# Output projection of a decoder block: seven products with sums replaced by eight plain ones, and two expert homes loaded earlier

## The chip, the cores and the metric

One core of one Trainium2 chip runs the whole program. The metric is the device time of one execution in microseconds, the median of the runs. All arithmetic is float32.

## What is computed

One decoder block on 256 tokens of width 1024, with a sparse attention (NSA) and a retention as token mixers and a mixture of 32 experts behind them. What matters here is the joint between the two halves:

```python
x = x + W_o( sigmoid(gA) * (yA @ W_upA) + sigmoid(gB) * (yB @ W_upB) )
x = x + HierMoE(RMSNorm(x))   # coarse top-1 group of 4, then top-2 of its 8 experts
```

Each of the 32 experts has gate and up weights of 1024x256 each (2 MB together) and down weights of 256x1024 (1 MB). All 32 are streamed from memory once per execution, 96 MB in all, whichever tokens chose them.

## The kernel before

**Order of the work.** The kernel is written by hand, one instruction stream for each engine, with semaphores between them. Each result of TensorE (PE) is a *job* in one of 8 PSUM banks; the list END_JOBS (L104) gives the bank of each job of the last part before the experts. A job is full when PE is done with it, and emptied when another engine has read it. The order of the calls in each engine's stream is the order in which it works; an engine that waits holds all that stands behind it.

**Token tiles and quarters.** The 256 tokens are two tiles of 128 (t = 0, 1), the 1024 columns two halves of 512 (n = 0, 1). A `product` (L693) is a sum over k-slices of 128: four matmuls of 128x128 by 128x512.

**Projections by seven products.** The gate and up projections (groups vr, gr, ga, gb, un, ur) and the output projection (out) each compute a 2x2 block product with seven products in place of eight (Winograd's form of Strassen's scheme). For it DVE makes four sums of weight quarters (T1 to T4) and four sums of quarters of the left operand, and further sums put the products together. In the group out the jobs are outX (first and second product), outZ (fifth), outW (sixth and seventh), outQ (fourth) and out3 with out4 (third product, in two pieces of 256 columns). ACT keeps the first product (`keep_first("out")`, L1396), POOL adds it to three quarters of x (L637 to L640), and DVE adds the others (L1940 to L1970). Token tile 1 comes ahead in the groups ur and out.

**Around it.** DVE's `merge(t, n)` (L1888) adds the two gated mixers in gate_a; PE transposes the result in four jobs mT00 to mT11 (`merged_transposes`, L1009), ACT copies them to mergedT (L1374), which lies in the region called keys. When a piece of x has its output sum, ACT sums its squares (L1400), POOL weights it for the experts (L628), PE transposes it in the jobs x2T00 to x2T12 (`stream_transposes`, L1051), and ACT copies them to h2T (L1410). PE's `route(t)` multiplies h2T with the router weights; DVE's `router(t)` (L1997) turns the logits into the tokens' choices by a chain of small operations; `places(t)` (PE L1065, DVE L1984) numbers the tokens of each expert. Then PE's `gather` (L1115) picks the tokens of the first four experts with a selection matrix, first from tile 0, then, after places(1) and counts, from tile 1.

**The experts.** Batches of four experts: gate and up products GU0 to GU3 (jobs GU0.c and on), tanh, products, down products O0.c and O1.c, and a combination into four PSUM banks which were seeded with x (`seed`, ACT L1422). Expert e's gate-up weights lie in home e mod 6, its down weights in home e mod 8 (L383 to L388). The homes are regions that the first half of the kernel uses for other things: ring slots, xs, x, keys, windows, qkT and others.

**The loads.** All large loads are issued from the queue of SyncE (SP), in one order, each behind a wait for its home (L465 to L529). `first_gu(e)` and `first_dw(e)` load expert e's weights into an empty home; `reload_gu(e)` waits until GU of expert e - 6 is full, `reload_dw(b)` until O0.c and O1.c of batch b - 2 are. The weights of the output projection lie in two blocks, out0 in ring slot 2 and out1 in the region vr_and_gr.

Of the kernel before, what the change touches and what calls it, by code (L numbers as in the profile page):

```python
# [12 lines left out]
P = 128  # L13
# [33 lines left out]
def shape_tables():  # L47

    def onehot(dist):
# [54 lines left out]
END_JOBS = [("urX", 3), ("urV", 4), ("urZ", 5), ("urW", 7), ("mT10", 2), ("mT11", 1), ("outX", 6), ("mT01", 0), ("mT00", 2),  # L104
            ("outZ", 5), ("outW", 7), ("outQ", 4), ("x2T10", 2), ("out3", 3), ("x2T00", 0), ("out4", 1), ("x2T01", 2),
            ("route0", 0), ("x2T11", 3), ("x2T12", 1), ("route1", 3), ("pos0", 2), ("pos1", 3), ("counts", 0)]
# [11 lines left out]


NTH = dict(vr=1, gr=2, ga=3, gb=4, un=5, ur=6, out=7)  # L120
# [28 lines left out]
def build(nc, a, out):  # L149
    with ExitStack() as ctx:  # L150
# [109 lines left out]
        mergedT = r_kpad[:, :].rearrange("p (k t) -> p k t", k=KT)  # L260
        ya_sums = q_and_ya[:, 0:1024].rearrange("p (s k n) -> p s k n", s=4, k=2)
        yr_sums = [attention[:, i * 512:(i + 1) * 512].rearrange("p (k n) -> p k n", k=4) for i in range(4)]
        second_aside = xs[:, :, :].rearrange("p t (k n) -> p (t k) n", k=2)

        m0 = nsa[:, 0:4096]
        selG = m0[:, 0:256].rearrange("p (t e s) -> p t e s", t=TT, e=BE)
        selW = m0[:, 256:512].rearrange("p (t e s) -> p t e s", t=TT, e=BE)
        selWT = m0[:, 512:768]
        hg = m0[:, 768:1792].rearrange("p (k s) -> p k s", k=KT)
        gu_sb = m0[:, 1792:2816].rearrange("p (b n) -> p b n", b=2)  # L270
# [3 lines left out]
        h2T = nsa[:, 2048:4096].rearrange("p (k t) -> p k t", k=KT)  # L274
# [7 lines left out]
        out_sums = [gate_a[:, t, n * 512:n * 512 + 512].rearrange("p (k n) -> p k n", k=4) for t, n in ((1, 0), (0, 1), (0, 0), (1, 1))]  # L282
# [39 lines left out]
        s_S, s_aS, s_rS, s_oS = sem("h_sums"), sem("attention_sums"), sem("retention_sums"), sem("merged_sums")  # L322
        s_x_P1, s_ga, s_gb = sem("first_product_added"), sem("attention_gate_tanh"), sem("retention_gate_tanh")
# [20 lines left out]
        def quarters(group):  # L344

            if group in ("ur", "out"):
                w = [slot(f"{dict(ur='upr', out='out')[group]}{i}").rearrange("p (k n) -> p k n", k=4) for i in range(2)]
# [7 lines left out]
        def left(v, one=0):  # L355

            n = v.shape[1] // 2
            a, b = (slice(t * P, (t + 1) * P) for t in (one, 1 - one))
            return v[:, 0:n, a], v[:, n:2 * n, a], v[:, 0:n, b], v[:, n:2 * n, b]
# [4 lines left out]
        def results(group):  # L364
# [4 lines left out]
            one = 1 if group == "ur" else 0  # L369
            return v[:, one, 0:512], v[:, one, 512:D], v[:, 1 - one, 0:512], v[:, 1 - one, 512:D]  # L370

        def piece_ready(piece):

            return dict(out0=(s_P7_read, NTH["out"]), out1=is_emptied("outW"), out2=is_emptied("outX"), out3=is_emptied("out3"),
                        out4=is_emptied("out4"))[piece]
# [51 lines left out]
        def _(sp):  # L427
# [42 lines left out]
            first_dw(2)  # L470
            sp.wait_ge(s_y, TT)
# [13 lines left out]
            first_dw(6)  # L485
            sp.wait_ge(s_P7, NTH["ur"])
# [74 lines left out]
        def _(pool):  # L561
# [93 lines left out]
        def _(pe):  # L655
# [327 lines left out]
            r11, r12, r21, r22 = left(yrT, 1)  # L983
# [28 lines left out]
            merged_transposes(1, 0, 1)  # L1012
# [4 lines left out]
            merged_transposes(1, 1, 2)  # L1017
            m11, m12, m21, m22 = left(mergedT, 1)
            b11, b12, b21, b22 = quarters("out")
            oX = begin("outX")  # L1020
            have("mT10")
            for b in ("out0", "out1"):
                pe.wait_ge(*loaded(b))
            product(oX[:, :], m11, b11, True, False).then_inc(s_P1, 1)
# [3 lines left out]
            merged_transposes(0, 1, 3)  # L1028
            have("mT11")
            pe.wait_ge(s_P1_kept, NTH["out"])  # L1030
            product(oX[:, :], m12, b21, False, False, range(2))
            merged_transposes(0, 0, 4)
            done("outX", product(oX[:, :], m12, b21, False, True, range(2, 4)))
            oZ = begin("outZ")
            pe.wait_ge(s_T1, NTH["out"])
            pe.wait_ge(s_oS, 1)
            done("outZ", product(oZ[:, :], out_sums[0], b12))
            oW = begin("outW")
            pe.wait_ge(s_oS, 2)
            pe.wait_ge(s_T2, NTH["out"])  # L1040
            product(oW[:, :], out_sums[1], second_aside, True, False).then_inc(s_P6, 1)
            oQ = begin("outQ")
            have("mT01")
            pe.wait_ge(s_T4, NTH["out"])
            done("outQ", product(oQ[:, :], m22, b21))
            pe.wait_ge(s_oS, 3)
            pe.wait_ge(s_T3, NTH["out"])
            pe.wait_ge(s_P6_read, NTH["out"])
            done("outW", product(oW[:, :], out_sums[2], b11, False, True))
# [28 lines left out]
            stream_transposes("x2T10")  # L1078
            o3, o4 = begin("out3"), begin("out4")
            pe.wait_ge(s_oS, 4)  # L1080
            done("out3", product(o3[:, 0:256], out_sums[3], b22[:, :, 0:256]))
            stream_transposes("x2T00")
            product(o4[:, 0:256], out_sums[3], b22[:, :, 256:512], True, False, range(2))
            stream_transposes("x2T01")
            done("out4", product(o4[:, 0:256], out_sums[3], b22[:, :, 256:512], False, True, range(2, 4)))
# [4 lines left out]
            stream_transposes("x2T12")  # L1090
# [150 lines left out]
        def _(act):  # L1241
# [52 lines left out]
            def keep_first(group):  # L1294

                act.wait_ge(s_P1, NTH[group])
                dst, scale = (x_squared, 0.5) if group == "out" else (results(group)[2], 1.0)
                nc.scalar.activation(dst, ps(f"{group}X")[:, :], ACT.Copy, scale=scale).then_inc(s_P1_kept, 1)
# [914 lines left out]
```

## Time and profile before

| | |
|---|---|
| median of 3 runs | 505.08 us (503.76 to 505.58) |
| the profiled execution | 502.69 us |
| its span in the profile | 500.7 us |
| PE busy | 469.1 us, 94% |
| DVE busy | 225.7 us, 45% |
| ACT busy, POOL busy | 89.9 us, 40.7 us |
| moved by DMA | 151.33 MB, mean 302 GB/s |
| mean granted clock of PE | 0.957 |

Each engine's busy time is the sum of its instructions; the span runs from the first instruction to the last. A busy PE need not be at full rate: the granted clock is 1.00 at 2.4 GHz and 0.50 at 1.2 GHz, and a float32 matmul shows as two instructions, so that a product of four k-slices is 8 in the views. Releasers of waits are inferred.

### The profile page before, as it was taken

Reading aid. Unit: us, or ns where it says so; the run is one execution under the profiler, and the core shown is the slowest. Engines: PE = TensorE matmul, PEld = TensorE weight load, DVE = VectorE, ACT = ScalarE, POOL = GpSimd, SP = SyncE. Lnnn points to the kernel's source line nnn. Section 1 sums busy time; section 2 is a strip of 40 time slices with the busy share of each in tenths; the row PEclk is TensorE's granted clock in tenths of the full one; section 3 lists DMA queues with packets and bytes.
Section 4 is the critical chain, followed back from the end, with each engine's and each line's share of the span. In section 5 each row is a group of like instructions: output and inputs, shape, how many; then the busy total and the mean of one; then the engine's idle time right before and its main releaser. Section 6 shows DMA issues by size and latency. Waiting matters only on the chain.

```text
span 500.7 us, 6261 instructions
## 1 busy us (share of the span) xinstructions
PE 469.1 (94%) x2434; PEld 259.2 (52%) x2434; DVE 225.7 (45%) x511; ACT 89.9 (18%) x244; POOL 40.7 (8%) x62
## 2 busy tenths in 40 slices
PE   5999999999999999999989889999999998979873
PEld 2499745564555545544435846464563636437320
DVE  1563019928766578779684651222231311111203
ACT  1000006214341110100101712021111211011012
POOL 0700050500000001000132300000000000000001
PEclk9999999999999999999989888999999996987987
DMA  8998679326025019489783989999999999999972
GB/s 262 418 377 206 207 283 375 130 61 277 0 84 254 0 63 418 191 346 418 276 344 111 395 327 429 400 428 428 407 432 414 426 427 408 431 408 432 417 292 88
DMA packets 20860, 151.33 MB, mean 302 GB/s; under 512 B 2947, under 2 KB 3396, under 8 KB 14172
## 3 DMA queue, kind: packets, MB, share of 16 engines
q1 hardware_dynamic: 19296, 147.88, 72.9%
q0 software_dynamic: 1296, 2.92, 2.9%
q8 instruction: 22, 0.36, 0.3%
q10 hardware_dynamic: 236, 0.08, 0.1%
q14 instruction: 10, 0.08, 0.0%
HBM read 148.25 MB, written 2.62 MB: 301 GB/s over the span
## 4 chain that ended last, share of the span: by engine, by line
PE 73%; DMA 17%; DVE 5%; SPq 2%; issue 2%; ACT 0%; POOLq 0%; POOL 0%; DVEq 0%; ACTq 0%
PE bank L672 33%; PE bank L697 29%; DMA ring<-in_moe_gate_up 10%; DMA attention_small<-in_moe_down 6%; PE bank L1127 4%; PE bank L1100 4%; PE bank L703 2%; SPq L453 1%; DMA ring<-in_dense 1%; SPq L457 1%; DVE ring L1616 0%; DVE nsa L1528 0%; DVE nsa L1890 0%; DVE nsa L1886 0%; DVE nsa L2068 0%
## 5 line engine op out<-in xcount | busy, mean ns | idle before, releaser
L2068 DVE COPY nsa<-bank 128x512 f32<-128x512 f32 x32 | 22.1, 691 | 97.3 <-PE bank L672 71.7
L697 PE MATMUL bank<-ring,x 128*128 128x512 f32 x128 | 57.3, 594 | 0.0
L672 PE MATMUL bank<-ring,nsa 128*32 128x512 f32 x336 | 43.1, 638 | 5.6 <-DMA ring<-in_moe_gate_up 5.6
L672 PEld LDWEIGHTS bank<-cst,nsa 128*128 128x128 f32 x256 | 34.4, 213 | 24.5 <-issue 16.6
L1462 ACT ACTIVATE nsa<-bank 128x512 f32<-128x512 f32 (+1 forms) x40 | 22.2, 554 | 127.3 <-PE bank L672 104.7
L697 PE MATMUL bank<-ring,hT_and_y 128*128 128x512 f32 x96 | 43.4, 597 | 0.0
L672 PE MATMUL bank<-cst,nsa 128*128 128x32 f32 x256 | 37.2, 298 | 1.2 <-DVE nsa L2068 1.2
L697 PEld LDWEIGHTS bank<-ring,x 128*128 128x128 f32 x128 | 23.8, 190 | 27.6 <-issue 27.5
L1127 PE MATMUL bank<-nsa,Tb 128*128 128x128 f32 x256 | 36.1, 308 | 1.0 <-DVE nsa L1994 1.0
L1127 PEld LDWEIGHTS bank<-nsa,Tb 128*128 128x128 f32 x256 | 35.4, 225 | 1.2 <-issue 1.2
L2078 DVE SCALAR_TENSOR_TENSOR cst<-cst,bank 128x64 f32<-128x64 f32 x32 | 7.1, 221 | 58.0 <-ACT cst L1470 58.0
L1100 PE MATMUL bank<-nsa 128*128 128x512 f32 x64 | 29.9, 607 | 0.8 <-ACT nsa L1462 0.8
L672 PE MATMUL bank<-hT_and_y,ring 128*128 128x256 f32 x128 | 28.2, 380 | 0.2 <-issue 0.2
L697 PEld LDWEIGHTS bank<-ring,hT_and_y 128*128 128x128 f32 x96 | 17.6, 190 | 20.1 <-issue 20.1
L672 PEld LDWEIGHTS bank<-hT_and_y,ring 128*128 128x128 f32 x128 | 24.1, 190 | 4.0 <-DVE hT_and_y L1547 0.8
L672 PEld LDWEIGHTS bank<-ring,nsa 128*32 128x32 f32 x336 | 9.5, 111 | 26.4 <-issue 20.1
L1699 DVE CUSTOM_DVE_ANT_0 nsa<-bank,Tb 128x128 f32<-128x128 f32 (+1 forms) x32 | 9.6, 354 | 28.9 <-DMA Tb<-bias_rows 26.9
L672 PE MATMUL bank<-ring,hT_and_y 128*128 128x128 f32 (+2 forms) x96 | 22.0, 388 | 0.0
L672 PE MATMUL bank<-ring,Tb 128*128 128x512 f32 x32 | 16.9, 688 | 5.3 <-DMA ring<-in_dense 5.3
L1100 PEld LDWEIGHTS bank<-nsa 128*128 128x128 f32 x64 | 11.3, 189 | 20.0 <-issue 19.5
L1274 ACT ACTIVATE nsa<-nsa,mneg 128x128 f32<-128x128 f32 (+1 forms) x32 | 14.1, 443 | 26.1 <-DVE mneg L1528 26.1
L651 POOL TENSOR_TENSOR st<-st 128x1 f32<-128x1 f32 x2 | 1.6, 778 | 208.8 <-DVE st L2134 208.8
(274 smaller groups left out, 690.8 us busy)
## 6 DMA issues: line engine op xcount, KB each, us to landing
ring<-in_moe_gate_up SPq DMA_DIRECT2D x21, 2048.0 KB, 19.6
ring<-in_dense SPq DMA_DIRECT2D x17, 2048.0 KB, 12.1
hT_and_y<-in_moe_gate_up SPq DMA_DIRECT2D x6, 2048.0 KB, 17.6
vr_and_gr<-in_moe_gate_up SPq DMA_DIRECT2D x5, 2048.0 KB, 22.7
windows<-in_moe_down SPq DMA_DIRECT2D x8, 512.0 KB, 17.9
nsa<-in_moe_down SPq DMA_DIRECT2D x8, 512.0 KB, 19.4
queries_and_attention<-in_moe_down SPq DMA_DIRECT2D x8, 512.0 KB, 24.3
attention_small<-in_moe_down SPq DMA_DIRECT2D x8, 512.0 KB, 19.4
```

The lines of the kernel that those rows point to most:

```text
L453: sp.dma_start(GU[i].rearrange("p k w f -> p (k w f)"), expert(gate_up_v, j, e)).then_inc(s_gu[i], 16)
L457: sp.dma_start(DW[i][:, h, :, :].rearrange("p k n -> p (k n)"), expert(down_v[:, h, :, :], j, e)).then_inc(s_dw[i][h], 16)
L672: return nc.tensor.matmul(o, l, r, start=s, stop=e)
L697: ins = nc.tensor.matmul(o, l[:, k, :], r[:, k, :], start=first and k == 0, stop=last and k == n - 1, skip_group_check=True)
L703: ins = nc.tensor.transpose(o[:, i * P:(i + 1) * P], s, ident)
L1100: return nc.tensor.matmul(bank[4 + q][:, 0:w], l, r, start=s, stop=e, skip_group_check=True)
L1127: ins = nc.tensor.matmul(o[:, k * P:(k + 1) * P], xe[:, t, (4 * h + k) * P:(4 * h + k + 1) * P], selG[:, t, :, :].rearrange("p e s -> p (e ...
L1274: ins = nc.scalar.activation(p, p, ACT.Exp, bias=mneg[:, t, h, b:b + 1], accum_out=sums[:, t, h, b:b + 1])
L1462: nc.scalar.activation(dst, bank[k][:, src], ACT.Copy).then_inc(emptied[k], 1)
L1699: ins = V.tensor_tensor_reduce(dst, o[:, b * S:b * S + w], Tt[:, h, S - w:S], 1.0, -3e38, ALU.add, ALU.max, mx[:, t, h, b:b + 1])
L2068: V.tensor_copy(dst, bank[k][:, src]).then_inc(emptied[k], 1)
L2078: V.scalar_tensor_tensor(h, t, 1.0, bank[k][:, 0:2 * C], ALU.add, ALU.mult).then_inc(s_hch, 1)
```

## The change

The output projection is computed piece by piece: for each of the pieces out0 (tile 0, columns 0 to 511), out1 (tile 0, the rest), out2 (tile 1, columns 0 to 511), out3 and out4 (tile 1, 256 columns each) the product over all eight k-slices, in two halves of four (`output`). The weight sums, the left sums, the kept first product and POOL's additions are gone, and so is the aside copy of a weight sum in xs. Tile 0 is now ahead in ur and out. mergedT lies in gate_b, each quarter where the gate quarter was, so the keys region is free after the retention and xs after the un group: the down weights of expert 3 (home keys) are loaded behind job Y11, and those of expert 4 (home xs) behind the first merge. The blocks out0 and out1 now hold column halves in place of row halves. The working area of the experts in nsa is laid out in another order.

Cut to its core:

```diff
@@ SP's queue @@
             first_dw(2)
+            sp.wait_ge(*is_full("Y11"))
+            first_dw(3)
             sp.wait_ge(s_y, TT)
...
             first_dw(6)
+            sp.wait_ge(s_mrg, 1)
+            first_dw(4)
             sp.wait_ge(s_P7, NTH["ur"])
...
             first_dw(1)
-            sp.wait_ge(s_P6, NTH["out"])
-            sp.wait_ge(s_T4, NTH["out"])
-            first_dw(4)
-            sp.wait_ge(*is_full("outW"))
+            sp.wait_ge(*is_full("out2"))
             first_gu(4)
-            sp.wait_ge(*is_full("outQ"))
-            sp.wait_ge(s_oS, 4)
-            first_dw(3)
             sp.wait_ge(*is_full("out4"))
             first_gu(5)
@@ POOL @@
-            pool.wait_ge(s_P1_kept, NTH["out"])
-            for t, c0 in ((0, 0), (0, 512), (1, 512)):
-                pool.wait_ge(s_x[t], 32)
-                xx = x[:, t, c0:c0 + 512]
-                pool.tensor_tensor(xx, xx, x_squared, ALU.add).then_inc(s_x_P1, 1)
             pool.wait_ge(s_nffn, 16)
+            weighted("out0")
+            weighted("out1")
+            router_rstd(0)
             weighted("out2")
-            weighted("out0")
-            router_rstd(0)
-            weighted("out1")
             weighted("out3")
@@ PE @@
-            merged_transposes(1, 1, 2)
-            product(oX[:, :], m11, b11, True, False).then_inc(s_P1, 1)
...
+            merged_transposes(0, 1, 2)
+            def output(o, t, kh, c0, c1):
+                w = cols(f"out{c0 // 512}", 512)[:, 4 * kh:4 * kh + 4, c0 % 512:c0 % 512 + c1 - c0]
+                return product(o[:, 0:c1 - c0], mergedT[t][kh], w, kh == 0, kh == 1)
+            o0 = begin("out0")
+            have("mT00")
+            pe.wait_ge(*loaded("out0"))
+            output(o0, 0, 0, 0, 512)
             pe.wait_ge(s_T4, NTH["ur"])
             pe.wait_ge(s_P7_read, NTH["ur"])
             done("urW", product(uW[:, :], r22, u21, False, True))
...
+            merged_transposes(1, 1, 3)
             have("mT01")
+            done("out0", output(o0, 0, 1, 0, 512))
+            o1 = begin("out1")
+            pe.wait_ge(*loaded("out1"))
+            output(o1, 0, 0, 512, D)
+            merged_transposes(1, 0, 4)
...
+            stream_transposes("x2T00")
+            done("out1", output(o1, 0, 1, 512, D))
+            o2 = begin("out2")
+            have("mT10")
+            output(o2, 1, 0, 0, 512)
             stream_transposes("x2T01")
+            have("mT11")
+            done("out2", output(o2, 1, 1, 0, 512))
             pe.wait_ge(s_wr, 1)
             have("x2T00", "x2T01")
             route(0, range(KT))
+            o3 = begin("out3")
+            output(o3, 1, 0, 512, 768)
+            stream_transposes("x2T10")
+            done("out3", output(o3, 1, 1, 512, 768))
+            o4 = begin("out4")
+            output(o4, 1, 0, 768, D)
+            places(0)
             stream_transposes("x2T11")
+            done("out4", output(o4, 1, 1, 768, D))
             have("x2T10")
             route(1, range(4))
             have("x2T11")
             route(1, range(4, 6))
+            stream_transposes("x2T12")
             have("x2T12")
             route(1, range(6, KT))
-            places(0)
@@ ACT @@
+            act.wait_ge(s_gb, 4)
             keep_first("ur")
+            merged_out(0, 0)
+            merged_out(0, 1)
+            merged_out(1, 1)
             merged_out(1, 0)
-            keep_first("out")
...
+            squares(0, "out0")
+            turned("x2T00")
+            squares(1, "out1")
+            turned("x2T01")
+            squares(2, "out2")
             turned("x2T10")
+            normed(0)
+            seed(1)
             squares(3, "out3")
             turned("x2T11")
+            exps_router(0)
             squares(4, "out4")
             turned("x2T12")
             seed(0)
+            normed(1)
             exps_router(1)
             seed(2)
             seed(3)
@@ DVE @@
-            first_sum_of_out()
-            second_sum_of_out()
             last_product("ur")
...
-            left_sums(mergedT, out_sums, s_oS, 1)
-            third_sum_of_out()
-            third_left_sum(mergedT, out_sums, s_oS, 1)
-            fourth_sum_of_out()
...
+            residual("out0")
+            residual("out1")
+            variance(0)
+            residual("out2")
             dve.wait_ge(s_ms, 2)
+            router(0)
+            residual("out3")
+            places(0)
+            residual("out4")
             partial_variance()
-            router(0)
             variance(1)
-            places(0)
             router(1)
             places(1)
```

## Rows read from the trace of the kernel before

**Rows 1.** The page's slices of 12.5 us: busy share of the DMA engines, and what they moved.

```profile
DMA  8998679326025019489783989999999999999972
GB/s 262 418 377 206 207 283 375 130 61 277 0 84 254 0 63 418 191 346 418 276 344 111 395 327 429 400 428 428 407 432 414 426 427 408 431 408 432 417 292 88
```

**Rows 2.** Stretches: us, busy time by engine, then clock, DMA share and GB/s.

```profile
287.30:289.40 2.10, 1.78 (x16) 1.69 (x16) 0.58 (x3) 1.00 (x2) 0.00 (x0) 0.99 0.17 35
294.40:483.00 188.60, 177.56 (x1260) 95.88 (x1264) 40.89 (x124) 28.12 (x70) 0.00 (x0) 0.92 1.01 419
483.00:500.60 17.60, 8.47 (x40) 2.14 (x32) 4.34 (x8) 4.07 (x10) 1.56 (x2) 0.79 0.26 100
```

**Rows 3.** SP's queue in order of time: start, us, issue.

```profile
243.96 0.33 SPq L453 DMA_DIRECT2D ring<-in_moe_gate_up  x1
...
288.33 0.80 SPq L457 DMA_DIRECT2D x<-in_moe_down  x2
...
292.73 0.33 SPq L453 DMA_DIRECT2D hT_and_y<-in_moe_gate_up  x1
...
312.24 0.33 SPq L457 DMA_DIRECT2D windows<-in_moe_down  x1
```

**Rows 4.** The chain that ended last, in order of time: start, us, what.

```profile
210.19 29.20 PE bank L697 x68
...
273.14 0.44 PE bank L703 x4
273.58 1.73 PE bank L697 x8
...
277.93 1.96 PE bank L672 x16
```

**Rows 5.** PE in order of time: start, us, group, and the pause ahead of it.

```profile
243.76 0.60 PE L703 MATMUL bank<-cst,nsa 128*128 128x128 f32 x4
...
255.34 0.66 PE L703 MATMUL bank<-cst,nsa 128*128 128x128 f32 x4 [1.95 <-DVE nsa L1890]
...
280.69 1.95 PE L672 MATMUL bank<-wr,nsa 128*128 128x36 f32 x16 [0.35 <-ACT nsa L1250]
...
284.08 3.58 PE L1127 MATMUL bank<-nsa,Tb 128*128 128x128 f32 x16 [0.70 <-DVE nsa L1994]
287.49 0.31 PE L672 MATMUL bank<-member,cst 128*128 128x32 f32 x2
...
288.79 2.02 PE L1127 MATMUL bank<-nsa,Tb 128*128 128x128 f32 x16 [0.32 <-DVE nsa L1994]
290.74 1.92 PE L672 MATMUL bank<-hT_and_y,nsa 128*32 128x512 f32 x16
```

**Rows 6.** Stretches around the half clock; third value from the end is the granted clock.

```profile
241.50:244.30 2.80, 2.80 (x11) 1.44 (x10) 0.40 (x2) 0.00 (x0) 0.00 (x0) 1.00 0.02 7
...
256.60:260.00 3.40, 3.40 (x5) 1.35 (x4) 3.21 (x3) 0.03 (x1) 0.00 (x0) 0.50 0.94 383
...
283.90:287.30 3.40, 3.22 (x15) 3.25 (x16) 2.70 (x16) 2.62 (x8) 0.00 (x0) 0.50 0.96 402
287.30:290.70 3.40, 3.08 (x27) 2.92 (x26) 0.58 (x3) 1.60 (x3) 0.00 (x0) 0.99 0.42 136
...
297.50:304.40 6.90, 6.90 (x36) 2.44 (x28) 1.43 (x5) 0.22 (x1) 0.00 (x0) 0.51 0.99 423
```

**Rows 7.** DVE in order of time: start, us, instruction.

```profile
240.87 0.69 DVE L1890 TENSOR_TENSOR nsa<-nsa 128x512 f32<-128x512 f32 x1
...
253.65 1.63 DVE L1890 TENSOR_TENSOR nsa<-nsa 128x512 f32<-128x512 f32 x1
...
275.35 0.42 DVE L1938 SCALAR_TENSOR_TENSOR x<-bank,x 128x256 f32<-128x256 f32 x1 [0.88 <-PE bank L697]
...
283.93 0.22 DVE L2003 SCALAR_TENSOR_TENSOR rt<-bank,st,rbias 128x4 f32<-128x4 f32 x1
...
286.51 0.25 DVE L2018 SCALAR_TENSOR_TENSOR member<-cst,rt 128x32 f32<-128x32 f32 x1
```

More of the change, by code:

```diff
@@ L102 @@
 BANK0 = 5
-END_JOBS = [("urX", 3), ("urV", 4), ("urZ", 5), ("urW", 7), ("mT10", 2), ("mT11", 1), ("outX", 6), ("mT01", 0), ("mT00", 2),
-            ("outZ", 5), ("outW", 7), ("outQ", 4), ("x2T10", 2), ("out3", 3), ("x2T00", 0), ("out4", 1), ("x2T01", 2),
-            ("route0", 0), ("x2T11", 3), ("x2T12", 1), ("route1", 3), ("pos0", 2), ("pos1", 3), ("counts", 0)]
+END_JOBS = [("urX", 3), ("urV", 4), ("urZ", 5), ("urW", 7), ("mT00", 2), ("mT01", 1), ("out0", 6), ("mT11", 0), ("out1", 5),
+            ("mT10", 2), ("x2T00", 1), ("out2", 4), ("x2T01", 3), ("route0", 0), ("out3", 1), ("x2T10", 2), ("out4", 3),
+            ("pos0", 1), ("x2T11", 0), ("route1", 0), ("x2T12", 2), ("pos1", 3), ("counts", 0)]
 PIECES = dict(out0=(0, 0, 512), out1=(0, 512, 1024), out2=(1, 0, 512), out3=(1, 512, 768), out4=(1, 768, 1024))
 TURNED = dict(x2T00=("out0", 0, 4), x2T01=("out1", 4, 8), x2T10=("out2", 0, 4), x2T11=("out3", 4, 6), x2T12=("out4", 6, 8))
-NTH = dict(vr=1, gr=2, ga=3, gb=4, un=5, ur=6, out=7)
+NTH = dict(vr=1, gr=2, ga=3, gb=4, un=5, ur=6)
 BATCH_C = ["GU0.c", "GU1.c", "T0.c", "GU2.c", "T1.c", "GU3.c", "T2.c", "T3.c", "WT.c"]
@@ L344, in quarters @@
         def quarters(group):
[L346 to L347 removed]
+            if group == "ur":
+                w = [slot(f"upr{i}").rearrange("p (k n) -> p k n", k=4) for i in range(2)]
                 return w[0][:, :, 0:512], w[0][:, :, 512:1024], w[1][:, :, 0:512], w[1][:, :, 512:1024]
@@ L353, in quarters, with left @@
             return w[0][:, 0:4, :], w[1][:, 0:4, :], w[0][:, 4:8, :], w[1][:, 4:8, :]
-        def left(v, one=0):
+        def left(v):
             n = v.shape[1] // 2
-            a, b = (slice(t * P, (t + 1) * P) for t in (one, 1 - one))
-            return v[:, 0:n, a], v[:, n:2 * n, a], v[:, 0:n, b], v[:, n:2 * n, b]
+            return [v[:, k * n:(k + 1) * n, t * P:(t + 1) * P] for t in range(TT) for k in range(2)]
         def weights_of(group):
@@ L368, in results @@
                 v = r_qkT[:, :].rearrange("p (t d) -> p t d", t=TT)
-            one = 1 if group == "ur" else 0
-            return v[:, one, 0:512], v[:, one, 512:D], v[:, 1 - one, 0:512], v[:, 1 - one, 512:D]
+            return v[:, 0, 0:512], v[:, 0, 512:D], v[:, 1, 0:512], v[:, 1, 512:D]
         def piece_ready(piece):
-            return dict(out0=(s_P7_read, NTH["out"]), out1=is_emptied("outW"), out2=is_emptied("outX"), out3=is_emptied("out3"),
-                        out4=is_emptied("out4"))[piece]
+            return is_emptied(piece)
         def dense(block):
@@ L1585, in _, with left_sums @@
                 freed(job, ins)
-            def left_sums(v, s, sums, one=0):
-                a11, a12, a21, a22 = left(v, one)
+            def left_sums(v, s, sums):
+                a11, a12, a21, a22 = left(v)
                 V.tensor_tensor(s[0], a21, a22, ALU.add).then_inc(sums, 1)
@@ L1925, in _ @@
             link(gate_up("ur", 2, c21))
-            merge(0, 0)
-            for j in ("mT10", "mT01", "mT00"):
-                dve.wait_ge(*is_emptied(j))
-            left_sums(mergedT, out_sums, s_oS, 1)
-            third_sum_of_out()
-            third_left_sum(mergedT, out_sums, s_oS, 1)
-            fourth_sum_of_out()
-            dve.wait_ge(*is_emptied("mT11"))
-            def residual(piece, job, t, c0, c1):
-                xx = x[:, t, c0:c1]
-                return V.scalar_tensor_tensor(xx, ps(job)[:, 0:c1 - c0], 0.5, xx, ALU.mult, ALU.add)
@@ L2180, in dense_rows @@
 def dense_rows(w_in, w1k, w1v, nsa_up, ret_up, w_out):
-    whole = dict(w1k=(w1k, 0, 16), w1v=(w1v, 0, 16), upn=(nsa_up, 0, 4), upr0=(ret_up, 0, 4), upr1=(ret_up, 4, 8),
-                 out0=(w_out, 0, 4), out1=(w_out, 4, 8))
+    whole = dict(w1k=(w1k, 0, 16), w1v=(w1v, 0, 16), upn=(nsa_up, 0, 4), upr0=(ret_up, 0, 4), upr1=(ret_up, 4, 8))
     made = []
@@ L2187, in dense_rows @@
             w, k0, k1, c0, c1 = w_in, 0, KT, *W_IN[b]
+        elif b in ("out0", "out1"):
+            c0 = 512 * int(b[3])
+            w, k0, k1, c1 = w_out, 0, KT, c0 + 512
         else:
```

170 lines of the change are left out of this document (35 added, 135 removed).

## The prediction

> **What bounds the kernel now.** I read the page's slices first [rows 1]: the DMA engines are loaded unevenly until slice 23 and at 9 tenths from there on, while PE is busy for 94% of the whole span. So the last 200 us are a stream of expert weights, and the question is what starts it. The stretches answer [rows 2]: from 294.4 to 483 us the DMA share is 1.01 at 419 GB/s, and behind it stand 17.6 us of tail. The stream feeds 32 experts of 2 MB gate-up and 1 MB down weights through 6 gate-up homes and 8 down homes; the first 20 MB can be fetched ahead, the other 76 MB (79.7e6 bytes) only as homes come free. 79.7e6 bytes at 419 GB/s is 190 us, and 292.73 us, where the first reload is issued, plus 190 is 483. The SP queue shows that this first reload is issued when the first expert's gate-up product is done [rows 3]. Before it the DMA engines had been idle: share 0.17 in 287.3 to 289.4 us [rows 2], so nothing queued was in the way. The end of the program is therefore the end of PE's first gate-up product (call it T, 292.7 us) plus about 208 us that the change does not touch. I price the change by what it does to T. The same queue holds a second condition: four reloads of 2 MB (8.39e6 bytes, 20.0 us at that rate) must last until the first down reload at 312.24 us [rows 3]; 292.7 + 20.0 is 312.7 and some 1 us of start-up, so there is little spare there.
>
> **The path to T.** Prices from the chain [rows 4]: 68 matmul instructions of 128x512 took 29.20 us, 0.429 each. A product of four k-slices is 8 of them, 3.43 us; four transposes 0.44; a product 256 columns wide 1.73; one token tile's router product 1.96. In PE's order of time [rows 5] two things delay it between 243.76 and 290.74 us: a pause of 1.95 us at 255.34, waiting for DVE's last merge, and short pauses from 280.3 on. After each of them the granted clock stands at 0.50, the lower of its two levels, 1.2 GHz, for some 3.4 us [rows 6]: 256.6 to 260.0, and 283.9 to 287.3.
>
> **Part 1, plain product for seven products.** Seven products become 2 token tiles x 2 column halves x 2 k-halves = 8: PE gains one, +3.43 us. Removed are four DVE weight sums, four left sums, ACT's kept first product, and three POOL additions. They cost PE only where it waited. The last merge (DVE) took 1.63 us [rows 7], where its twin at 240.87 us took 0.69. In the new order PE has work until that merge is needed: half of out0 (3.43), the last ur product, mT11, the other half of out0 and half of out1. The merge would be done by 255.3 us even at the old price and is needed at 258.4. So the 1.95 us pause goes, and with it its slow stretch, which cost half of 3.4, 1.7 us. Balance: 3.43 - 1.95 - 1.7 = -0.2 us. If that cover were gone, the price would be the pause again.
>
> **Part 2, the order, step by step.** From 243.76 us [rows 5], with the prices above: mT01 to 244.20, out0 first half 247.63, last ur product 251.06, mT11 251.50, out0 254.93, out1 first half 258.36, mT10 258.80, x2T00 259.24, out1 262.67, out2 first half 266.10, x2T01 266.54, out2 269.97, route0 271.93, out3 first half 273.66, x2T10 274.10, out3 275.83, out4 first half 277.56, places(0) about 0.2, x2T11 277.98, out4 279.71, twelve of sixteen router instructions 281.18, x2T12 281.40. Its last four wait for ACT's copy of x2T12; the nearest row is the 0.35 us that route1 waited for such a copy [rows 5], bounds 0.2 (its share of a handoff) and 0.9 (a 0.6 us square ahead of it on ACT). I take 0.4. Route1 ends at 282.3 us, against 280.69 + 1.95 = 282.64 before: -0.3. Residuals and squares for out0 to out3 each have at least one product of PE time to hide in; the one of out4 takes 0.42 us [rows 7] and is covered by the twelve router instructions.
>
> Then the gain proper. Before, DVE did places(0) ahead of the second router, which began at 283.93 and had its members at 286.76 [rows 7], 2.83 us. Now places(0) is done at about 278.5, and the second router begins when route1 is full, at 282.4: its members are ready at 285.3, 1.5 us earlier (0.3 of it from route1, 1.2 from the place in DVE's order). Before, PE came to places(1) only at 287.49, for its first gather of 16 instructions ran at half clock, 3.58 us against 2.02 for the second [rows 5]; now that gather starts at 282.3 and is over before 285.3, so PE is there 0.15 us (a handoff) behind the members and another 0.6 us goes. places(1), counts and DVE's selection take 1.3 us as before (287.49 to 288.79). The second gather starts at 286.7 instead of 288.79: T moves by **-2.1 us**.
>
> **Part 3, the clock on the new path.** PE now pauses about 1.1 us in front of places(1) and 0.3 behind it, with only small products between. Before the clock fell at 283.9 PE had done much the same: router and place products with pauses of 0.35 and 0.70 us [rows 5, 6]. Bounds: nothing is given back, or a whole slow stretch, 1.7 us. I take the price of the row nearest to it, the gather that ran at half clock: 3.58 - 2.02 = +1.56 us. It would now fall on the second gather and the first gate-up product, with nothing to hide it. A rule of the Trainium skill, page "TensorE: Matmul & The Clock Gate", section "Why this matters for your kernels", asks only that long idle gaps between bursts be avoided; by it these short pauses would cost nothing and the sum would stay at -2.1. The trace does not quite agree: short pauses stood ahead of the half clock at 283.9.
>
> **Part 4, the loads.** Two loads of 1 MB (2.5 us of stream each) are moved on SP's queue. The one into the keys home goes behind Y11 (about 195 us), ahead of the loads of out1, upr1 and out0, into a slice followed by one that moved 191 GB/s only [rows 1]. out1 is later by at most 2.5 us, and is needed at 255 us: nothing. The one into xs goes to the first merge (241.6 us), in front of the gate-up load of 243.96 [rows 3]; the DMA share is 0.02 there [rows 6], so that load is later by under 1 us and is needed after 292 us: nothing. The two gate-up loads of 2 MB that wait for out2 and out4 are issued at 270.0 and 279.7 and land by 285; the last down load, after the seeds, at 288.33 us before [rows 3] and at about 286.2 now, lands by 289. All homes are full before T, as before, so the earlier loads buy nothing by themselves. The nsa layout moves no work.
>
> **Sum.** T: -0.2 - 0.1 (rest of the order) - 1.2 (router behind places) - 0.6 (late places) + 1.56 (clock) = **-0.5 us**. The profiled execution took 502.69 us with a span of 500.7; it becomes 502.2. The median of the runs is 505.08, 2.4 us above the profiled one; I carry the same difference to it: **504.5 us**. A measurement of this kernel can tell about 0.5%, 2.5 us.
>
> **Rivals.**
> (A) Forecast, 504.5: one slow stretch falls on the gather or gate-up product before T. For it: [rows 6]; against it: where the stretch falls may differ from run to run.
> (B) The clock stays at full until T: 505.08 - 2.1 = 503.0. This is also what the skill's rule gives. For it: 287.3 to 290.7 held a pause of 0.32 us and the same small products, and the clock stayed at full behind it, and the first gate-up product ran in 1.92 us [rows 5, 6].
> (C) Slower. The half clock holds for two stretches on end, as it did from 297.5 to 304.4 us [rows 6], and both lie before T, or the second one stretches the first batch until the four reloads run dry before the down reload. 6.9 us at half clock costs 3.4: -2.1 + 3.4 = +1.3, 506.4. It decides once half-clock time ahead of T is over 4.2 us. Against it: before, the clock was back at full from 287.3 on.
> (D) The stream is set by its total and not by T: 2 MB moved to idle time (DMA share 0.02) save 2.1e6 / 419 GB/s = 5.0 us, 500.1. Against it: DMA was idle before T, so 2 MB were never in its way.
> (E) The change does not do what it says: mT10 or a copy comes late and PE pauses all the same. It then has 3.43 more and keeps 1.95 + 1.7, 3.65 over A: 508.2. Against it: 3 us of slack by the working above.
>
> **Chances.** A 0.48, B 0.30, C 0.11, D 0.06, E 0.05. The range runs from 501.3 to 507.0: down from B by the runs' own spread (503.76 to 505.58) and part of the way to D, up past C by as much; left out are D, E and the edges of the others, some 2 in 10. Faster by over 0.5% (under 502.55) takes D, half of B and a little of A: 0.22. Slower by over 0.5% (over 507.6) takes E and the edge of C: 0.10. Within: 0.68.
>
> **What the new profile would show.** No pause of PE near 255 us and a clock of 1.00 from 244 to 280; 64 matmul instructions of 512-wide cost in the output stage and none on DVE over 128x2048 there; route1 ending near 282.3; second router members near 285.3; second gather at 286.7, first reload on SP's queue at 290.6 (B) or 292.2 (A); DMA share 1.0 from 1.5 us after it, for 189 us. The time follows that reload one for one. I am wrong if the reload moves and the end does not, if a gate-up load is still in flight at T, or if PE waits in the output stage for DVE or ACT by more than 1 us in all.

## The result and the profile after

The changed kernel takes 500.35 us, median of 14 runs (498.89 to 504.40), against 503.30 us for the kernel before, 14 runs beside them (501.30 to 505.61): ratio 0.9945, 95% interval 0.9924 to 0.9966, or 2.8 us less (1.7 to 3.8). Measured again on another chip it was 0.9966 (0.9939 to 0.9992). The forecast of 504.5 us was too high and its range began above the median: two steps failed, the base and the clock. Slow executions (two in all, of the kernel before) are left out of all ratios and means.

The profiled execution took 500.49 us with a span of 498.7, 2.0 less than before. SP's queue of the changed kernel, in order of time, shows the first reload and the first down reload (start, us, issue):

```profile
290.62 0.33 SPq L446 DMA_DIRECT2D hT_and_y<-in_moe_gate_up  x1
...
306.88 0.33 SPq L450 DMA_DIRECT2D windows<-in_moe_down  x1
```

The first reload was at 292.73 us before [rows 3], so it moved by 2.1 us, and the span by 2.0: behind it stand 208.1 us here and 208.0 there. PE of the changed kernel in order of time (start, us, group, pause ahead of it):

```profile
251.41 3.60 PE L683 MATMUL bank<-ring,nsa 128*128 128x512 f32 x8
254.84 3.60 PE L683 MATMUL bank<-vr_and_gr,nsa 128*128 128x512 f32 x8
258.28 0.60 PE L689 MATMUL bank<-cst,nsa 128*128 128x128 f32 x4
...
281.57 0.63 PE L658 MATMUL bank<-wr,nsa 128*128 128x36 f32 x4 [0.47 <-ACT nsa L1230]
282.04 2.03 PE L1107 MATMUL bank<-nsa,Tb 128*128 128x128 f32 x16
285.30 0.38 PE L658 MATMUL bank<-member,cst 128*128 128x32 f32 x2 [1.24 <-DVE member L1933]
...
286.68 2.02 PE L1107 MATMUL bank<-nsa,Tb 128*128 128x128 f32 x16 [0.33 <-DVE nsa L1909]
288.63 1.92 PE L658 MATMUL bank<-hT_and_y,nsa 128*32 128x512 f32 x16
```

The pause of 1.95 us of [rows 5] is gone; mT10 stands at 258.28 us without one. The second gather begins at 286.68 (forecast 286.7, before 288.79), and both gathers take 2.0 us. Stretches of the changed kernel, with the columns of [rows 6]:

```profile
256.60:260.00 3.40, 3.40 (x15) 1.93 (x14) 0.00 (x0) 1.08 (x3) 0.56 (x1) 1.00 0.94 389
282.00:290.70 8.70, 7.14 (x62) 5.28 (x65) 5.01 (x27) 3.65 (x10) 0.00 (x0) 1.00 0.91 362
...
292.30:481.00 188.70, 172.66 (x1260) 91.01 (x1264) 40.91 (x124) 28.11 (x70) 0.00 (x0) 0.95 1.01 420
481.00:498.70 17.70, 8.98 (x40) 2.14 (x32) 4.34 (x8) 4.07 (x10) 1.54 (x2) 0.79 0.24 90
```

The clock is 1.00 in the places where it stood at 0.50 before (256.6 to 260.0 us, and around the first gather), and the stream behind is that of [rows 2], 420 GB/s in place of 419. DVE's last gating and merge in the changed kernel:

```profile
251.90 0.69 DVE L1839 SCALAR_TENSOR_TENSOR nsa<-nsa,qkT 128x512 f32<-128x512 f32 x1
252.63 0.69 DVE L1843 TENSOR_TENSOR nsa<-nsa 128x512 f32<-128x512 f32 x1
```

They take 0.69 us each; the merge took 1.63 before [rows 7].

### The profile page after: what moved, and what is told of

It is laid out like the page before. It is cut to its first block, busy times and chain, and to the rows that moved or that the text cites. A ratio compares the mean times of both kernels' runs of the same rounds, so it can differ in the third digit from the quotient of the medians.

```text
span 498.7 us, 6263 instructions
## 1 busy us (share of the span) xinstructions
PE 464.1 (93%) x2450; PEld 255.2 (51%) x2450; DVE 210.0 (42%) x499; ACT 89.4 (18%) x243; POOL 34.5 (7%) x59
## 4 chain that ended last, share of the span: by engine, by line
PE 56%; DMA 29%; SPq 6%; DVE 4%; issue 2%; POOL 1%; ACT 0%; POOLq 0%; DVEq 0%; ACTq 0%
PE bank L683 30%; PE bank L658 18%; DMA ring<-in_moe_gate_up 11%; DMA bias_rows<-etab 9%; DMA attention_small<-in_moe_down 6%; SPq L450 3%; PE bank L1080 3%; PE bank L1107 3%; PE bank L689 2%; DMA x<-in_x 2%; SPq L446 2%; DMA Tb<-bias_rows 1%; DVE ring L1593 0%; SPq L431 0%; DVE nsa L1505 0%
## 5 line engine op out<-in xcount | busy, mean ns | idle before, releaser
L658 PEld LDWEIGHTS bank<-cst,nsa 128*128 128x128 f32 x256 | 32.0, 200 | 23.5 <-issue 17.2
L683 PEld LDWEIGHTS bank<-ring,x 128*128 128x128 f32 x128 | 23.8, 190 | 27.6 <-issue 27.5
L658 PE MATMUL bank<-cst,nsa 128*128 128x32 f32 x256 | 34.7, 286 | 1.2 <-DVE nsa L1980 1.2
L1107 PE MATMUL bank<-nsa,Tb 128*128 128x128 f32 x256 | 32.4, 288 | 0.3 <-DVE nsa L1909 0.3
L1107 PEld LDWEIGHTS bank<-nsa,Tb 128*128 128x128 f32 x256 | 31.6, 204 | 0.4 <-issue 0.4
L658 PE MATMUL bank<-ring,Tb 128*128 128x512 f32 x32 | 16.3, 668 | 5.2 <-DMA ring<-in_dense 5.2
L1230 ACT ACTIVATE nsa<-bank 128x384 f32<-128x384 f32 (+2 forms) x25 | 11.6, 517 | 43.2 <-PE bank L689 43.1
```

The lines of the kernel that those rows point to most:

```text
L658: return nc.tensor.matmul(o, l, r, start=s, stop=e)
L683: ins = nc.tensor.matmul(o, l[:, k, :], r[:, k, :], start=first and k == 0, stop=last and k == n - 1, skip_group_check=True)
L1107: ins = nc.tensor.matmul(o[:, k * P:(k + 1) * P], xe[:, t, (4 * h + k) * P:(4 * h + k + 1) * P], selG[:, t, :, :].rearrange("p e s -> p (e ...
L1230: freed(job, nc.scalar.activation(dst, src, ACT.Copy, scale=scale))
```

## The experiments

All ratios are to the kernel before, run beside. "First reload" is the first gate-up reload on SP's queue, and "half clock" a granted clock near 0.50. Each run left one profile, of one of its executions. e1 to e4 shared one chip, e5 to e8 another, e9 to e11 a third; e7 and e12 are single executions, e12 on a fourth chip.

**The pause put back (e1).** In PE's stream of the changed kernel:

```diff
             merged_transposes(1, 1, 3)
+            merged_transposes(1, 0, 4)
             have("mT01")
...
             output(o1, 0, 0, 512, D)
-            merged_transposes(1, 0, 4)
```

> The changed kernel with one step moved: PE does the transposes mT10 ahead of the second half of out0, where DVE's last merge is not done, so that the pause of the kernel before (about 1.9 us near 251 us) is back and nothing else is. Theory 1 (a pause of this size is followed by a stretch at the lower clock, and the end follows the first reload one for one): pause 1.9 us, clock 0.50 for about 3.4 us behind it, first reload and end later by 1.9 + 1.7 = 3.6 us against the changed kernel. Theory 2 (the pause alone is paid): +1.9 us and clock 1.00. Theory 3 (the end does not hang on the first reload): no change of the time.

Ratio 1.0012 (0.9982 to 1.0041), 503.34 us: the whole gain is gone. PE and one stretch of e1:

```profile
253.29 0.66 PE L689 MATMUL bank<-cst,nsa 128*128 128x128 f32 x4 [1.80 <-DVE nsa L1843]
...
288.60 3.36 PE L1107 MATMUL bank<-nsa,Tb 128*128 128x128 f32 x16 [0.32 <-DVE nsa L1909]
```

```profile
253.30:260.00 6.70, 6.70 (x19) 3.34 (x20) 0.69 (x1) 1.32 (x3) 1.29 (x1) 1.00 0.96 380
```

The pause is there, but the clock behind it stays at 1.00, against theory 1. It fell later instead, on the second gather (3.36 us), where the forecast had put it. The first reload came at 294.13 us, 3.5 later than in the changed kernel: 1.9 of pause and 1.6 of clock. The span is 2.3 us longer than the changed kernel's, and the median 2.6 longer than that of e4 on the same chip (500.75 us), which is the changed kernel but for two loads. The pause is paid; its slow stretch is not tied to it. Theory 3 falls.

**One more product (e2).**

```diff
             output(o1, 0, 0, 512, D)
+            output(o1, 0, 0, 512, D)
```

> The changed kernel with one more product: the first half of out1 is computed twice (the second one overwrites the first), 8 matmul instructions of 0.429 us. Theory 1 (end = first reload + 208 us): first reload and end later by 3.4 us, so about 0.7 us over the kernel before. Theory 3 (the stream of expert weights is set by its total, and time in front of it is free): 0. It also gives one more look at the clock in the stretch of the gathers, 282 to 294 us: forecast was 0.50 somewhere in it; rival 1.00.

Ratio 1.0036 (1.0009 to 1.0063), 505.02 us: against the two ratios of the changed kernel (0.9945, 0.9966) 0.8% or 4 us slower, for 3.4 us of PE. The first reload is at 295.74 us, 5.1 later than in the changed kernel and 208.2 us ahead of the end of its span, so the end follows the first reload. Here too the clock fell, in the middle of the second gather and on into the first gate-up product (2.79 and 2.77 us in place of 2.02 and 1.92), which is 1.6 us of the 5.1.

**places(0) back behind the second router product (e3).**

```diff
             output(o4, 1, 0, 768, D)
-            places(0)
...
             route(1, range(6, KT))
+            places(0)
```

and on DVE `places(0)` behind `variance(1)`.

> The changed kernel with places(0) back behind the second router product on PE and behind variance(1) on DVE, as in the kernel before. Theory 1: the second router starts 0.8 to 1.2 us later, and the first reload and the end with it by as much; if the clock falls on the first gather as before, 0.6 us more. Rival: DVE's order is not on the path, 0.

Ratio 0.9981 (0.9948 to 1.0014), 502.60 us, which is 1.9 longer than e4 on the same chip; the intervals of the two ratios overlap. PE of e3:

```profile
281.31 0.63 PE L658 MATMUL bank<-wr,nsa 128*128 128x36 f32 x4 [0.47 <-ACT nsa L1230]
281.78 0.39 PE L658 MATMUL bank<-member,cst 128*128 128x32 f32 x2
282.87 2.86 PE L1107 MATMUL bank<-nsa,Tb 128*128 128x128 f32 x16 [0.70 <-DVE nsa L1909]
...
287.41 3.58 PE L1107 MATMUL bank<-nsa,Tb 128*128 128x128 f32 x16
```

The expectation was half wrong. DVE's second router began at 282.64 us, only 0.3 later than the 282.32 of the changed kernel, not 0.8 to 1.2. But the pause of 0.70 us ahead of the first gather is back, the clock falls 1 us into that gather and is still down for the second one, and the first reload comes at 292.90 us, 2.3 later. In the kernel before, DVE came to places(0) late, because the first router's product ran only at 277.93 us [rows 4], where the changed kernel has it at 269.89. DVE of the kernel before, from the members of tile 0 to the second router at 283.93 us [rows 7]:

```profile
282.60 0.25 DVE L2018 SCALAR_TENSOR_TENSOR member<-cst,rt 128x32 f32<-128x32 f32 x1
...
283.42 0.19 DVE L1986 TENSOR_TENSOR posm<-bank,posm 128x32 f32<-128x32 f32 x1 [0.15 <-PE bank L672]
283.64 0.29 DVE L1994 TENSOR_TENSOR nsa<-cst,posm 128x128 f32<-128x128 f32 x1
```

So the lateness of the first router and the 1.1 us of places(0) and the variance behind it held the second router back together; with the first router early, places(0) is worth 0.3. places(0) ahead in the order of before was not run.

**The loads back late (e4).** `first_dw(4)` behind out1, `first_dw(3)` behind out2:

```diff
-            sp.wait_ge(*is_full("Y11"))
-            first_dw(3)
...
-            sp.wait_ge(s_mrg, 1)
-            first_dw(4)
...
+            sp.wait_ge(*is_full("out1"))
+            first_dw(4)
             sp.wait_ge(*is_full("out2"))
             first_gu(4)
+            first_dw(3)
```

> The changed kernel with the two down loads back late: that of xs behind out1, that of keys behind out2 and the gate-up load. Theory 1 (all homes are full before the first reload anyway): 0, within 0.3 us, first reload at the same time. Rival (2 MB moved out of the stream's way is what the change brings): slower by up to 2.1e6 bytes / 419 GB/s = 5.0 us.

Ratio 0.9963 (0.9932 to 0.9995), first reload at 290.65 us, span 498.6 against 498.7. The earlier loads bring nothing that shows; rival D falls.

**The changed kernel again (e5).**

> The changed kernel itself once more, on the chip of the runs beside it. Its profile is one more look at the stretch from 282 us on: so far the clock fell ahead of the first reload in two of four kernels that have the same instructions there. Theory 1 (the clock falls in some executions and not in others, by where the pauses happen to lie): either result, with the first reload at 290.6 or near 292.1 us. Ratio to the kernel before as at first, 0.9945 within 0.3%.

Ratio 0.9966 as above. First reload 291.15 us, of which 0.54 came from ahead of the stage (its first gather began that much later); clock 1.00 up to it. Its span was 502.0 all the same, 210.9 behind the reload. Two stretches of e5 bear on it:

```profile
294.50:303.50 9.00, 9.00 (x50) 3.80 (x49) 1.98 (x7) 0.85 (x3) 0.00 (x0) 0.62 0.99 379
482.00:491.00 9.00, 7.19 (x34) 1.64 (x34) 0.28 (x2) 1.50 (x4) 0.00 (x0) 0.62 0.23 92
```

The clock fell in the first batch and again in the tail, behind the stream. That this made the span long is argued and not shown: e11 also had a low clock behind its stream (0.70 over its last 17 us, against 0.71 over the last 20 us of e5), and its span ends 208.4 us behind the reload.

**POOL's additions moved, seven products kept (e6).** One line in the kernel before:

```diff
             pool.wait_ge(s_P1_kept, NTH["out"])
+            pool.wait_ge(s_oS, 4)
```

> The kernel before with one wait more: POOL's three additions to x wait for DVE's fourth left sum of the output group, so that they no longer run beside DVE's last gating and merge. Theory 1 (the pause of 1.95 us at 255 us came from DVE taking 1.62 and 1.63 us for those two in place of 0.69, because POOL ran beside it): both take 0.69 us, the pause is under 0.2 us, no clock of 0.50 behind it, first reload earlier by 1.9 us, or by 3.6 where the clock had fallen; the time then equals the changed kernel's within 0.3%, so the plain product is not what brings the gain. Rival (the two were slow for another reason, or the additions now delay the residuals): pause still there or moved, no gain.

Ratio 0.9961 (0.9934 to 0.9988), beside 0.9966 of the changed kernel on the same chip: as far as the intervals tell, one wait does as much as the whole change. DVE and POOL of the kernel before:

```profile
251.99 1.62 DVE L1886 SCALAR_TENSOR_TENSOR nsa<-nsa,qkT 128x512 f32<-128x512 f32 x1
```

```profile
248.51 6.22 POOL L640 TENSOR_TENSOR x<-x,hidden_partial 128x512 f32<-128x512 f32 x3 [50.05 <-ACT hidden_partial L1298]
```

DVE, POOL, PE and one stretch of e6:

```profile
251.71 0.69 DVE L1887 SCALAR_TENSOR_TENSOR nsa<-nsa,qkT 128x512 f32<-128x512 f32 x1
252.44 0.69 DVE L1891 TENSOR_TENSOR nsa<-nsa 128x512 f32<-128x512 f32 x1
```

```profile
261.76 3.71 POOL L641 TENSOR_TENSOR x<-x,hidden_partial 128x512 f32<-128x512 f32 x3 [63.58 <-DVE nsa L1602]
```

```profile
253.18 0.66 PE L704 MATMUL bank<-cst,nsa 128*128 128x128 f32 x4
...
277.56 2.11 PE L673 MATMUL bank<-wr,nsa 128*128 128x36 f32 x16 [0.35 <-ACT nsa L1251]
```

```profile
278.00:289.00 11.00, 10.11 (x52) 9.87 (x52) 5.58 (x30) 6.77 (x18) 0.56 (x1) 0.55 0.82 326
```

In the kernel before, the three additions ran from 248.51 us for 6.22 us, beside DVE; in e6, where they no longer run beside those two, they take 3.71, and DVE's two operations take 0.69 each in place of 1.62 and 1.63. PE has no pause at 253 us and reaches the second router product at 277.56, 3.1 us ahead of [rows 5]. Of these, 0.3 us come from ahead of the stage and 1.6 are the half clock that the first profile had and e7 and e12 (below) had not. From the product behind the transposes at 251 us to that router product it is 26.3 us in e6 and 27.6 in e7 and e12, so the wait itself is worth 1.3 us: a new pause of 0.36 us, for POOL's late additions, takes part of the 1.95 back. The Trainium skill, page "SBUF — State Buffer", section "SBUF: two separate sides", says that a GpSimd operation that reads SBUF and a VectorE operation with two SBUF inputs want the same port pair, which the one that starts first holds for the whole instruction while the other is blocked. The rows of POOL and of DVE agree. Then the lead is lost: the clock is at 0.55 from 278 to 289, and the first reload comes at 291.78 only, no earlier than in e7 and about where e12 has it. So the pause and its cause are shown, but this profile does not show where the gain in the median comes from.

**The kernel before, two more profiles (e7, e12).**

> The kernel before itself, one look. Theory 1 (the clock falls by chance of place): the pause of 1.95 us is there, and the clock behind it may be 0.50 or 1.00; first reload 292.7 where both slow stretches are there, down to 290.3 where none is. Rival (the slow stretches belong to the code): both at the same places as in the first profile.

> The kernel before, one more look, for the count of slow stretches. Theory 1 (with places(0) behind the second router product PE makes four short pauses around it, and the clock has fallen on the first gather in each of five looks with that order): 0.50 on the first gather again, second gather 4.8 us behind the first, first reload at 290.6 us or, where the clock falls behind the pause of 1.95 us too, near 292.5. Rival (chance alone): 1.00 on the first gather.

PE and two stretches of e7:

```profile
254.76 0.66 PE L703 MATMUL bank<-cst,nsa 128*128 128x128 f32 x4 [1.94 <-DVE nsa L1890]
...
281.93 3.57 PE L1127 MATMUL bank<-nsa,Tb 128*128 128x128 f32 x16 [0.70 <-DVE nsa L1994]
```

```profile
254.60:261.00 6.40, 6.24 (x18) 2.92 (x19) 4.89 (x6) 0.60 (x1) 0.00 (x0) 1.00 0.94 357
282.00:285.60 3.60, 3.60 (x19) 3.60 (x19) 2.44 (x15) 2.83 (x9) 0.00 (x0) 0.53 0.87 364
```

The same pause, 1.94 us, and no fall behind it; in e12 (pause 1.95, first gather 3.75 us) the same. But in e12 the clock had fallen earlier, in the second router product, and stayed down for 6.7 us (280.8 to 287.5). PE and stretches of e12:

```profile
279.12 2.15 PE L672 MATMUL bank<-wr,nsa 128*128 128x36 f32 x16 [0.35 <-ACT nsa L1250]
...
282.74 3.75 PE L1127 MATMUL bank<-nsa,Tb 128*128 128x128 f32 x16 [0.70 <-DVE nsa L1994]
```

```profile
280.00:282.00 2.00, 1.83 (x12) 1.62 (x11) 1.46 (x8) 1.87 (x6) 0.23 (x1) 0.68 1.12 471
282.00:284.00 2.00, 1.30 (x7) 1.29 (x7) 1.72 (x10) 1.42 (x5) 0.33 (x1) 0.50 1.02 426
284.00:286.00 2.00, 2.00 (x11) 2.00 (x11) 1.34 (x8) 1.67 (x4) 0.00 (x0) 0.50 0.82 352
286.00:288.00 2.00, 1.91 (x12) 1.83 (x10) 0.58 (x3) 0.87 (x2) 0.00 (x0) 0.61 0.11 37
```

First reload 290.65 and 291.89 us, spans 498.0 and 499.3. Theory 1 holds for the pause; chance alone does not hold for the first gather, which ran at half clock in both.

**Matmuls in the pause (e8, e11).**

```diff
                             if t == 1:
+                                o = begin("pos1")
+                                for _ in range(8):
+                                    mm(o[:, 0:P], tri, ident, True, True)
                                 places(1)
```

> The changed kernel with eight needless matmuls of 128x128 by 128 columns (0.11 us each) in the pause ahead of places(1), into the bank that pos1 overwrites. Theory 1 (the pauses there are what lets the clock fall): clock 1.00 up to the first reload, first reload at 290.6 us in every look, time that of the changed kernel less what its executions lose on the mean, 0.5 to 0.8 us. Rival (the clock falls there for the small products, whatever stands between): 0.50 in some looks, no gain.

> The changed kernel with the filler alone once more, on the chip of the two beside it. Theory 1: clock 1.00 from the first gather to the first reload again, ratio 0.9937 within 0.3%. Rival: 0.50 ahead of the first reload this time.

Ratios 0.9937 (0.9912 to 0.9961) and 0.9941 (0.9917 to 0.9964). PE of e8:

```profile
282.47 2.03 PE L1110 MATMUL bank<-nsa,Tb 128*128 128x128 f32 x16
284.34 1.95 PE L658 MATMUL bank<-cst 128*128 128x128 f32 x16
...
287.43 2.02 PE L1110 MATMUL bank<-nsa,Tb 128*128 128x128 f32 x16 [0.32 <-DVE nsa L1912]
```

The clock stays at 1.00 up to the first reload in both, at 291.37 and 290.83 us. Each of the eight matmuls shows as two instructions, so the filler took 1.9 us of PE where some 1 us was meant, and PE comes to places(1) 0.4 us later behind the first gather than in the changed kernel. The ratios are the lowest measured, but their intervals overlap those of the changed kernel (0.9945 and 0.9966): that it is faster is not shown.

**Two versions built on this (e9, e10).** e9 is e6 with the filler; e10 is e8 with the transposes x2T12 one step earlier:

```diff
             route(1, range(4))
+            stream_transposes("x2T12")
             have("x2T11")
             route(1, range(4, 6))
-            stream_transposes("x2T12")
```

> The kernel before (seven products) with POOL's additions late, as in the run before, and the eight needless matmuls ahead of places(1). Theory 1 (with the pause gone the seven products keep their lead of 3.4 us on PE, and only half-clock stretches ahead of the first reload hide it): where the clock stays at 1.00, first reload at 288.6 to 289.1 us, 1.5 to 2 us ahead of the changed kernel, ratio 0.990 to 0.994. The pauses of 0.35, 0.2 and 0.7 us around the second router product remain, so 0.50 may still come there in some looks. Rival (as good as the changed kernel at best): 0.9945 or more.

> The changed kernel with the filler and with the transposes x2T12 ahead of two of the k-slices of the second router product, so that ACT's copy is covered. Theory 1: the wait of 0.47 us before the last four router instructions shrinks to about 0.2, first reload 0.3 us earlier than with the filler alone, 290.3; ratio near that of the filler, 0.9937, less 0.0006. Rival: the residual of out4 is late and the pause moves ahead of x2T12, 0.

e9 missed its 0.990 to 0.994: it measured 0.9992 (0.9968 to 1.0015), although it holds the wait of e6. The first gather ran at half clock (3.42 us) and the filler, behind it, then kept PE from places(1) until 286.43 us; first reload 291.67. e10 did on PE what was expected, the wait of 0.47 us is gone and the first reload is at 290.18 us, the earliest of all. Its ratio was expected below that of the filler alone and is not: 0.9953 (0.9926 to 0.9980) beside 0.9941 of e11 on the same chip, which the intervals do not tell apart.

**The profiles side by side.** The second column has the half clock ahead of the first reload, by operation and with its total length. The numbers in brackets are executions.

| kernel | half clock ahead of the first reload | first reload | span | mean clock of its executions |
|---|---|---|---|---|
| before | behind the pause; first gather: 6.8 us | 292.73 | 500.7 | 0.964 (34), 0.963 (27), 0.963 (29) |
| e7 (before) | first gather: 3.4 us | 290.65 | 498.0 | |
| e12 (before) | second router product to first gather: 6.7 us | 291.89 | 499.3 | |
| e6 (seven products) | second router product to second gather: 9.9 us | 291.78 | 501.8 | 0.966 |
| e9 (seven products) | first gather: 3.4 us | 291.67 | 500.3 | 0.967 |
| e3 (places back) | both gathers: 7.0 us | 292.90 | 502.8 | 0.968 |
| changed, e4, e5 | none | 290.62, 290.65, 291.15 | 498.7, 498.6, 502.0 | 0.974, 0.971, 0.975 |
| e1 | second gather: 3.4 us | 294.13 | 501.0 | 0.971 |
| e2 | second gather and first gate-up product: 3.4 us | 295.74 | 503.9 | 0.975 |
| e8, e10, e11 (filler) | none | 291.37, 290.18, 290.83 | 499.6, 497.5, 499.2 | 0.976, 0.974, 0.974 |

## Why the prediction was wrong, and where it was right

**What bounds the kernel** was right. In all profiles but three the span ends 206.9 to 208.6 us behind the first reload; e3, e5 and e6 have 209.9 to 210.9, for reasons that stay open. One reading under it was wrong: the idle DMA engines of 287.3 to 289.4 us lie more than 3 us ahead of the first reload, and they are busy again up to it, with the last down load and a smaller one, issued from 288.33 us on. Stretches of the kernel before:

```profile
290.00:291.00 1.00, 1.00 (x12) 0.78 (x14) 0.15 (x1) 0.55 (x1) 0.00 (x0) 1.00 1.01 401
...
294.00:295.00 1.00, 0.38 (x4) 0.00 (x0) 0.93 (x5) 0.55 (x1) 0.00 (x0) 1.00 0.59 193
```

The conclusion stands even so: the dip at 294 us reads as those loads running out before the reload's own bytes come, and e1, e2 and e4 bear it out. "There is little spare" at the first down reload was right too, but small: where the clock fell in the first batch, as before, the down reload stood 19.5 us behind the first reload, against 16.3 in the changed kernel, and e6 lost an estimated 0.6 us of stream there: 392 and 356 GB/s in the two stretches of 3 us from 19 us on, against 410 and 418 in the changed kernel. It does not explain the long spans: e10 had the same 19.5 us and a span that ends 207.3 us behind its first reload.

**Part 1** gave -0.2 us and was right for the profiled pair, by luck. The product costs 3.4 us (e2), the pause of 1.95 goes, and why it was there is now known (e6). The 1.7 us for a slow stretch behind it is a wrong term for the median: such a pause stood in four profiles (before, e1, e7, e12) and the clock fell behind one of them. Against e7 or e12 this part would have been 3.43 - 1.95 = +1.5 us, not -0.2.

**Part 2** was right in its sum, step for step: the last router instructions ran from 281.57 (forecast route1 done at 282.3), the second members were ready at 285.15 (285.3), the second gather began at 286.68 (286.7), the wait for x2T12's copy came to 0.47 us (0.4). The cause named for the 1.2 us, places(0) ahead of the second router, was only a part of it: e3 measures 0.3 for its place alone, and the rest needs the first router to run 8 us earlier.

**Part 3 is the step that failed.** "I take the price of the row nearest to it" put +1.56 us into the sum for a half clock ahead of T, and the changed kernel had none: both its gathers took 2.0 us and its clock was 1.00. Its profiled execution took 500.49 us where 502.2 was forecast, 1.7 less, which is about this term. The place and the size were right where the clock did fall, 3.36 us for the second gather in e1, but that was in two of five profiles with this order (e1, e2; not in the changed kernel, e4, e5). Taken as one frequency this makes a mean charge of some 0.6 us. The two falls were, however, both in altered kernels whose gathers start 1.9 and 3.5 us later, and none was in the three that have its timing (the changed kernel, e4, e5); five profiles cannot tell chance from this. And the row I took it from was the wrong neighbour: the order of before, with a pause of 0.35 or 0.47 us at the second router product and one of 0.70 us ahead of the first gather, had the clock down on the first gather in six profiles of six (before, e3, e6, e7, e9, e12), the new order in none of five, nor in the three with the filler. So the new order did not put a slow stretch where none had been; it removed one that stood in each of those six. The pauses are not shown to be the cause: in e6 and e12 the clock was down before the pause of 0.70 us came. Rival B, 2.1 us less, was the case that came, and 2.1 lies inside the measured 1.7 to 3.8. That it fits the median is partly luck, for it was reckoned from a profile of the kernel before that had more half clock than e7.

**The base** failed as well. 505.08 us was a median of three; over 14 runs the same kernel has 503.30. The step was "2.4 us above the profiled one; I carry the same difference to it": over 14 runs the difference is 0.6. With -2.1 on that base the forecast would be 501.2, with -0.5 502.8. So 1.8 us of the miss are the base and 1.6 the clock; the rest, under 1 us, is inside the interval.

**Part 4** was right (e4). The load into xs was issued at 234.25 us rather than 241.6, to no effect. Of the rivals, C and E did not come and D is refuted by e4; but half clock of 6.7 us and more ahead of the first reload, as C had it, does occur (e3, e6, e12).

**What stays open.** The single profiles do not account for the whole mean gain. The kernel before has first reloads of 292.73, 290.65 and 291.89 us in its three profiles, on the mean only 0.9 later than the changed kernel's two, where its time is 1.7 to 2.8 us longer; e7 was level with the changed kernel in its first reload, and its span was 0.7 us shorter. The mean clock of all executions points the same way as the order argument: by an estimate from it, 0.963 before is 37 us at half clock in an execution of 500 (2 x 0.037 x 500), 0.974 is 26, and e3, e6 and e9, which have before's order around the gathers, lie between. In the profiles the stretch ahead of the first reload accounts for about half of those 11 us: 5.6 us on the mean of the three before, none in the changed kernel's two. Where the rest lies in an average execution is not known, since only one execution of each run leaves a trace.

## What to carry to other kernels

Ask of an engine's wait why the operation that ends it takes so long before paying work to hide it: here an operation of POOL beside one of DVE with two SBUF inputs made the pause, and one wait in POOL's stream (0.9961) could not be told in its time from a rewrite of the stage (0.9966). In front of a saturated stream count what moves the first free home; moving two loads ahead of it changed nothing that shows (e4). A clock stretch that shows in one profile has a frequency, not a price: take several profiles before it goes into a sum, and take the base from more than three runs.

## What had not been expected of the hardware

The clock fell more surely among small products with small pauses (router products 36 columns wide and gathers of 128, pauses of 0.17 to 0.70 us, six profiles of six) than behind one pause of 1.8 to 1.95 us ahead of products 512 columns wide (one of four). Once down it stayed down for 3.4 us in most profiles, but for 6.7 in e12, 7.0 in e3 and 9.9 in e6, with PE busy for most of that time. In three profiles of three it stayed at full with needless matmuls of 128 columns in the gap ahead of places(1), against three of five without them, which is too few to call the matmuls the reason.
